# Starting the hybrid mixers from unnormed x, with fp32r forget gates: a six-layer transformer stack on one core

## The reference, cut to what matters

```python
x = x + hybrid_mixer(rms_norm_2(x, mix_norm[l]), w_in[l], lb_all[l], hgrn_out_norm[l], fox_f_bias[l], w_out[l])

z = h @ w_in                       # 1024 x 3592, h = x * rsqrt(mean(x*x) + eps) * mix_norm
hq, hf, hi, hg, fq, fk, fv, ff = split(z)          # 4 x 512, 3 x 512, 8
logf_h = logaddexp(log(lb), log1p(-lb) + log_sigmoid(hf))
k_h = (1 - lb) * sigmoid(-hf)
o_h = hgrn2_chunk_scan(silu(hq), k_h, hi, logf_h)  # 4 heads, gated linear attention
o_h = rms_norm_2(o_h, out_norm_w) * silu(hg)
logf_f = log_sigmoid(ff + fox_bf)
o_f = forgetting_attention(fq, fk, fv, logf_f)     # 8 heads, causal softmax with decay
return concat(o_h, o_f) @ w_out
```

## Time and profile before

| | |
|---|---|
| median of 3 runs | 2643.28 us (2640.35 to 2643.76) |
| profiled execution | 2639.53 us, its span 2637.8 us |
| mean granted TensorE clock | 0.997 of 2.4 GHz |
| TensorE busy | 2578.1 us, 98% of the span |
| VectorE, ScalarE, GpSimd busy | 63%, 51%, 6% |
| hybrid 0 / hybrid 1 begin | at about 1601 / 2183 us of the span |

### The profile page before, as it was taken

One profiled execution on the slowest core, in us unless ns is written; L12 is line 12 of the kernel. 1 busy time (PEld: TensorE's weight loads), 2 busy tenths in 40 slices (PEclk: granted clock), 3 DMA queues, 4 the chain that ended last, 5 costly groups with the idle time before them and its releaser, 6 DMA issues.

```text
span 2637.8 us, 48807 instructions
## 1 busy us (share of the span) xinstructions
PE 2578.1 (98%) x21538; PEld 2516.6 (95%) x21538; DVE 1668.8 (63%) x1988; ACT 1357.2 (51%) x1687; POOL 163.0 (6%) x259
## 2 busy tenths in 40 slices
PE   8999999999999999999999999999999999999998
PEld 8989999899998999999999999999999999999998
DVE  5667556575586655676646656756656657764764
ACT  5745445554456544665535445555445436544543
POOL 4400000000020000420000000000000000000000
PEclk9999999999999999999999999999999999999999
DMA  7515565456554664533666765444766755344763
GB/s 215 170 33 160 193 239 164 144 180 224 181 168 148 193 240 148 155 122 118 206 240 171 195 225 169 135 154 136 198 195 185 196 194 161 113 136 138 195 196 128
DMA packets 430995, 452.43 MB, mean 172 GB/s; under 512 B 14114, under 2 KB 395792, under 8 KB 428608
## 3 DMA queue, kind: packets, MB, share of 16 engines
q1 hardware_dynamic: 417952, 416.05, 50.6%
q0 software_dynamic: 8336, 32.87, 3.6%
q10 hardware_dynamic: 4496, 0.39, 0.1%
HBM read 441.15 MB, written 7.60 MB: 170 GB/s over the span
## 4 chain that ended last, share of the span: by engine, by line
PE 85%; DVE 6%; ACT 6%; DMA 1%; issue 1%; POOL 1%; ACTq 0%; SPq 0%; DVEq 0%
PE ps L621 84%; ACT wH L1517 2%; DVE wL L2167 2%; ACT hidden_parts L1577 1%; DMA ring<-in_gdn_w_in 0%; DVE arena L2742 0%; ACT L1544 0%; POOL arena L508 0%; PE ps L1052 0%; DVE hT L2423 0%; POOL arena L510 0%; PE ps L1270 0%; DVE sq L2250 0%; DVE arena L2431 0%; DMA arena<-leaf_out 0%
## 5 line engine op out<-in xcount | busy, mean ns | idle before, releaser
L2167 DVE TENSOR_TENSOR wL<-ring,wH 128x2048 fp32r<-128x2048 f32 x392 | 898.6, 2293 | 744.6 <-ACT wH L1517 744.2
L1517 ACT ACTIVATE wH<-ring 128x2048 fp32r<-128x2048 f32 x392 | 753.6, 1922 | 988.8 <-PE ps L621 986.6
L621 PE MATMUL ps<-hidden_parts,wH 128*128 128x256 f32 x6656 | 989.5, 277 | 3.8 <-ACT hidden_parts L1577 2.8
L621 PEld LDWEIGHTS ps<-hidden_parts,wH 128*128 128x128 f32 x6656 | 899.6, 188 | 5.9 <-issue 3.6
L621 PE MATMUL ps<-hidden_parts,wL 128*128 128x256 f32 x3328 | 693.2, 276 | 1.5 <-DVE wL L2167 1.5
L621 PEld LDWEIGHTS ps<-hidden_parts,wL 128*128 128x128 f32 x3328 | 521.9, 188 | 1.8 <-DVE wL L2167 1.8
L621 PE MATMUL ps<-hH,wH 128*128 128x256 f32 x2624 | 366.1, 281 | 6.4 <-DVE hH L2184 3.1
L621 PE MATMUL ps<-hH,wL 128*128 128x256 f32 x2624 | 358.9, 278 | 3.5 <-DVE wL L2167 3.5
L621 PE MATMUL ps<-hL,wH 128*128 128x256 f32 x2624 | 347.7, 279 | 0.0
L621 PEld LDWEIGHTS ps<-hH,wH 128*128 128x128 f32 x2624 | 329.1, 189 | 12.6 <-issue 10.5
L621 PEld LDWEIGHTS ps<-hH,wL 128*128 128x128 f32 x2624 | 326.9, 188 | 4.3 <-DVE wL L2167 4.3
(11 more groups left out here) (324 smaller groups left out, 1971.7 us busy)
## 6 DMA issues: line engine op xcount, KB each, us to landing
ring<-in_mlp_w SPq DMA_DIRECT2D x128, 1024.0 KB, 5.4
ring<-in_ffn_w_gate SPq DMA_DIRECT2D x88, 512.0 KB, 4.0
ring<-in_ffn_w_up SPq DMA_DIRECT2D x88, 512.0 KB, 5.3
ring<-in_ffn_w_down SPq DMA_DIRECT2D x44, 1024.0 KB, 5.0
ring<-in_gdn_w_in SPq DMA_DIRECT2D x32, 1024.0 KB, 5.9
ring<-in_w_in SPq DMA_DIRECT2D x28, 1024.0 KB, 5.4
hidden_parts<-mem_parts POOLq DMA_DIRECT2D x14, 1024.0 KB, 6.9
ring<-in_mlstm_w_in SPq DMA_DIRECT2D x12, 1024.0 KB, 5.3
```

What stands on the lines that cost most here:

```text
L621: return pe.matmul(o, l, r, start=start, stop=stop, **k)
L1517: f(wH[:, n % PARTS, :], ring[:, n % RING, :], ACT.Copy).then_inc(sem("high_split"), 1)
L2167: tt(wL[:, n % PARTS, :], ring[:, n % RING, :], wH[:, n % PARTS, :].bitcast(F32), ALU.subtract)\
```

## The change

Both hybrid parts begin as cross does. `late_start` (ScalarE) copies x times the norm weights to fp32r and `late_low` (VectorE) makes its low part, in `start_x`, two stretches of the arena that later hold `gate` and `v_tok`. The first four slabs and the forget gates are made from start_x; the sum of squares is finished between the products of the second slab (`behind_high`). Products of the four slabs are multiplied by rs as VectorE takes them out of their banks (`scaled_out`, instead of ScalarE's copies; Silu is then done in place). The normed h, high and low, is made later (`normed`, `normed_high`, `normed_low`), for the fifth slab on. The forget gates become an fp32r product of three parts with the gate columns split (`fox_w`), multiplied by rs before the bias. The fifth slab's low half stands ahead of the forget gate's chain in VectorE's order, no longer behind the rows. In hybrid 0 all 48 filler matmuls go before the first product. POOL clears the upper part of `gate` only when the fourth slab is done.

```diff
         floorH, floorL = hH[:, 0, :], hL[:, 0, :]
+        start_x = (hidH[:, 24:32, :], hidH[:, 16:24, :])
+        fox_w = [flat_parts[:, at:at + DC * 8].rearrange("p (c n) -> p c n", c=DC) for at in (15424, 15488)]
         x_rows = v_tok
...
...
                     W.chain(pool.memset(qk[64:128, 12:16, :], 0.0))
+                    pool.wait_ge(sem("products_done"), group("w_in_2", i, HYBRID_ORDER[3]))
                     W.chain(pool.memset(gate[0:64, 4:8, :], 0.0))
...
...
-            def first_products(name, layer, js, c, at, src=(hH, hL), together=True):
+            def first_products(name, layer, js, c, at, src=(hH, hL), together=True, behind_high=None):
...
...
                     both_halves(1, high_w[1], xL, k)
+                if behind_high:
+                    behind_high()
                 pe.wait_ge(sem("low_split"), n[1] + 1)
...
...
             def hybrid(l):
-                norm_sum(behind=6, filler=filled_before[("hybrid", l)], at=(0, 0, 0, 0, 10))
-                first_products("w_in_2", l, HYBRID_ORDER[0:2], DC, columns)
+                fill(filled_before[("hybrid", l)], 0, 2 * MEM_PIECES)
+                first_products("w_in_2", l, HYBRID_ORDER[0:2], DC, columns, src=start_x,
+                               together=False, behind_high=summed_norm)
                 filler_out(filled_before[("hybrid", l)])
...
-                        pe.wait_ge(sem("gates_in"), GATE_LOADS)
-                        for k in range(DC):
-                            last = mm(ps[0:8, 0, 0:T], gw[:, 3 + l, k, 0:8], hT[:, k, :], k == 0, k == DC - 1)
+                        pe.wait_ge(sem("gate_split"), W.next("gate_split"))
+                        last = three(ps[0:8, 0, 0:T], [lambda k: fox_w[0][:, k, :], lambda k: fox_w[1][:, k, :]],
+                                     [lambda k: start_x[0][:, k, :], lambda k: start_x[1][:, k, :]], DC)
                         last.then_inc(sem("gates_done"), 1)
                     if n >= 4:
-                        pe.wait_ge(sem("evac"), W.next("evac"))
-                    (to_tokens if s in (4, 5) else to_channels)("w_in_2", l, s, bank_of(n))
+                        pe.wait_ge(sem("scaled_out"), W.next("scaled_out"))
+                    if n == 4:
+                        pe.wait_ge(sem("normH_ready"), W.next("normH_ready", 4))
+                        pe.wait_ge(sem("normL_ready"), W.next("normL_ready", 4))
+                    (to_tokens if s in (4, 5) else to_channels)("w_in_2", l, s, bank_of(n),
+                                                                src=start_x if n < 4 else (hH, hL))
                 to_channels("w_in_2", l, 8, 1)
...
...
                 empty_filler(filler)
+
+            def late_start(name, layer, j, gain, k0, filler):
+                for c in range(4):
+                    act.wait_ge(sem("x_ready"), W.next("x_ready"))
+                    for k in (2 * c, 2 * c + 1):
+                        ins = f(start_x[0][:, k, :], xT[:, k, :], ACT.Copy, scale=column(gain, k0 + k))
+                    ins.then_inc(sem("hH_ready"), 1)
+                empty_filler(filler)
+                split(slab_no[(name, layer, j)] + PARTS)
+                for c in range(4):
+                    f(sq[:, 2 * c:2 * c + 2, :], xT[:, 2 * c:2 * c + 2, :], ACT.Square).then_inc(sem("xsq_ready"), 1)
+                ln_exp()
+                act.wait_ge(sem("ss_ready"), W.next("ss_ready"))
+                rsqrt(ps[:, 2, 0:T], rs[:, :], D, "rs_ready")
+
+            def normed_high():
+                for c in range(4):
+                    act.wait_ge(sem("h_ready"), W.next("h_ready", 2))
+                    f(hH[:, 2 * c:2 * c + 2, :], hT[:, 2 * c:2 * c + 2, :], ACT.Copy).then_inc(sem("normH_ready"), 1)
...
...
             def hybrid(l):
-                x_norm("w_in_2", l, HYBRID_ORDER[0], filler=filled_before[("hybrid", l)])
-                channels("w_in_2", l, 1, 4, chunks(qk, 4))
-                act.wait_ge(sem("evac"), W.next("evac", 2))
+                late_start("w_in_2", l, HYBRID_ORDER[0], "mix_norm_2", l * DC, filled_before[("hybrid", l)])
+                for n in range(2):
+                    ready("w_in_2", l, HYBRID_ORDER[n])
+                act.wait_ge(sem("scaled_out"), W.next("scaled_out", 2))
                 W.chain(f(glog, qk[:, 4:8, :], ACT.Abs))
...
                 f(glog, glog, ACT.Ln, bias=1.0).then_inc(sem("glog_ready"), 1)
+                normed_high()
                 act.wait_ge(sem("fz_ready"), W.next("fz_ready"))
...
...
                 f(qk[:, 4:8, :], qk[:, 4:8, :], ACT.Sigmoid, scale=-1.0).then_inc(sem("hk_ready"), 1)
-                channels("w_in_2", l, 0, 6, chunks(qk, 0), func=ACT.Silu)
+                for s in range(2):
+                    ready("w_in_2", l, s)
+                    act.wait_ge(sem("scaled_out"), W.next("scaled_out"))
+                    v = qk[:, 2 * s:2 * s + 2, :]
+                    f(v, v, ACT.Silu)
                 channels("w_in_2", l, 3, 4, chunks(gate, 0), func=ACT.Silu)
...
...
                         attention_slab(SLAB_ENDS[n - 1])
-                W.next("evac", 12)
                 square_pair(0, two(ps[:, 0, :]), "o_ready")
...
...
-            def late_low(gain, k0, x_parts, name, layer):
+            def late_low(gain, k0, x_parts, name, layer, j=0):
                 for c in range(4):
...
                     ins.then_inc(sem("hL_ready"), 1)
-                split(slab_no[(name, layer, 0)] + PARTS)
+                split(slab_no[(name, layer, j)] + PARTS)
                 sum_squares("xsq_ready", "xsq_summed")
+
+            def normed(gain, k0):
+                for c in range(DC):
+                    stt(hT[:, c, :], xT[:, c, :], column(gain, k0 + c), rs[:, :], ALU.mult, ALU.mult)\
+                        .then_inc(sem("h_ready"), 1)
+
+            def normed_low():
+                dve.wait_ge(sem("h_ready"), W.next("h_ready", DC))
+                for c in range(4):
+                    dve.wait_ge(sem("normH_ready"), W.next("normH_ready"))
+                    v = slice(2 * c, 2 * c + 2)
+                    tt(hL[:, v, :], hT[:, v, :], hH[:, v, :].bitcast(F32), ALU.subtract)\
+                        .then_inc(sem("normL_ready"), 1)
...
...
             def hybrid(l):
-                x_norm("mix_norm_2", l * DC, "w_in_2", l, HYBRID_ORDER[0])
+                late_low("mix_norm_2", l * DC, start_x, "w_in_2", l, HYBRID_ORDER[0])
+                dve.wait_ge(sem("gates_in"), GATE_LOADS)
+                W.chain(dve.tensor_copy(fox_w[0], gw[:, 3 + l, :, 0:8]))
+                tt(fox_w[1], gw[:, 3 + l, :, 0:8], fox_w[0].bitcast(F32), ALU.subtract).then_inc(sem("gate_split"), 1)
                 if l == 0:
...
                 r = lambda k: rows[0:8, k, :]
+
+                def scaled_out(n):
+                    s = HYBRID_ORDER[n]
+                    dve.wait_ge(sem("products_done"), group("w_in_2", l, s))
+                    c = 2 * s if s < 2 else 4 + 2 * (s - 2)
+                    tt(qk[:, c:c + 2, :], two(ps[:, 4 + n, :]), rs_twice(), ALU.mult).then_inc(sem("scaled_out"), 1)
+
+                refill("w_in_2", l, HYBRID_ORDER[0])
+                dve.wait_ge(sem("rs_ready"), W.next("rs_ready"))
+                scaled_out(0)
+                scaled_out(1)
+                normed("mix_norm_2", l * DC)
                 refill("w_in_2", l, 3)
                 dve.wait_ge(sem("gates_done"), W.next("gates_done"))
-                ts(r(1), ps[0:8, 0, 0:T], gbias[:, 2 + l:3 + l], None, ALU.add).then_inc(sem("fz_ready"), 1)
+                W.chain(tt(r(1), ps[0:8, 0, 0:T], rs[0:8, :], ALU.mult))
+                ts(r(1), r(1), gbias[:, 2 + l:3 + l], None, ALU.add).then_inc(sem("fz_ready"), 1)
+                normed_low()
+                refill("w_in_2", l, 0)
                 dve.wait_ge(sem("glog_ready"), W.next("glog_ready"))
...
...
                 negative_cum(r(5)).then_inc(sem("rows_ready"), 1)
-                refill("w_in_2", l, 0)
+                scaled_out(2)
+                scaled_out(3)
                 if l:
```

## The result

| | before | after |
|---|---|---|
| median of 8 runs each, us | 2644.47 (2640.35 to 2648.22) | 2651.58 (2648.12 to 2652.96) |
| profiled execution, us (span) | 2639.53 (2637.8) | 2648.12 (2646.4) |
| mean granted clock | 0.997 | 0.993 |

The changed kernel is slower: ratio 1.0027, 95% interval 1.0017 to 1.0037, or 7.1 us between the medians. The forecast was +8.2 us (2651.5). The interval goes from 4.5 to 9.8 us, so the times alone don't tell the forecast from its rival without a fall of the clock (+4.8); the traces and experiment 2 have to. That 2651.5 lies within 0.1 of the median is partly luck: the change was 1.1 smaller than forecast, and eight runs put the kernel before 1.2 higher than the three that the forecast started from.

A forecast was written before the change was run, and what follows sets the result against it. The prediction took VectorE's queue up to the sixth slab's low half to set the pace: 3.5 in hybrid 1, 1.3 in hybrid 0 and 3.4 for the clock make +8.2 on 2643.3, 2651.5 us; range 2645 to 2656.

The forecast's parts named there:

- rival without a fall of the clock: Both hybrids: the low clock falls into the pauses or not at all; +4.8 us, 2648.1; chance 0.26.
- The start: Start of each hybrid: first product 1.77 us behind the residual, as in cross; worth 5.6 and about 3.6 of TensorE's time.
- The gates: Forget gates: 24 fp32r matmuls take 2.7 us, ceiling 5.4; neither end matters to the sum if VectorE sets the pace.
- VectorE's queue, hybrid 1: Walk of VectorE's instructions from rs to the sixth slab's low half, ending at 2227.3 against 2223.77.
- The term +3.5: Hybrid 1: the sixth slab's low half ends 3.5 us later than before.
- Hybrid 0: Sixth low half ends at 1645.9, where TensorE started on it at 1644.6 before: 1.3 us later.
- The waits: TensorE at the sixth slab: stands 4.7 us in hybrid 0; some 5 in hybrid 1, then again after 16 matmuls.
- The clock: Behind each hybrid's pause the granted clock falls to 1.2 GHz: 2 x 1.7 = 3.4 us, bounds 0 and 5.
- The sum: Whole kernel: +4.8 us from the later sixth low halves plus 3.4 for the clock, +8.2, 2651.5 us.
- moved fifth low half: VectorE's queue, hybrid 1: 2.2 us behind a wait of 0.9; the stretch after the first forget instruction loses those 2.2.
- moved clears: POOL's clearing waits for the fourth slab; used only by the attention, nothing sooner queued behind it, so no cost.

The follow-up runs named there:

- experiment 2: Changed kernel with matmuls of ones, whose result nothing uses, filling TensorE's pauses ahead of the sixth slab and its low half; 2646.52 us, ratio 1.0015 to the kernel before.
- experiment 5: Kernel before with the changed forget gates alone, keeping its normed start and its lists; 2639.03 us, ratio 0.9988 to the kernel before.
- experiment 7: Changed kernel with the forget gates' matmuls done twice and GpSimd's clears waiting for two more slabs' products; 2646.49 us, ratio 1.0020 to the kernel before.
- experiment 1: Changed kernel with the 24 forget-gate matmuls done twice in each hybrid part; 2655.87 us, ratio 1.0039 to the kernel before.
- experiment 9: Changed kernel with the fifth low half back behind the rows and GpSimd's clears behind two more slabs' products; 2643.74 us, ratio 1.0003 to the kernel before.
- two variants: Changed kernel with the gates' matmuls done twice (ratio 1.0039), and changed kernel with the fifth low half back behind the rows (ratio 1.0026).
- experiment 8: Kernel before with the changed forget gates, old normed start, and slab halves put in order of need; 2643.01 us, ratio 1.0004 to the kernel before.
- experiment 4: Changed kernel with slab halves made in the order TensorE needs them on ScalarE and VectorE; 2635.50 us, ratio 0.9969 to the kernel before.
- experiments 5 to 8: Old start with new gates (0.9988); changed kernel with fifth low half back (1.0026); gates twice, clears later (1.0020); old start, halves in order (1.0004).

## Why the prediction was right, point by point

- **The start.** Forecast +1.77 behind the residual, by cross; measured +1.77. rs forecast at +12.8 and +17.7, measured +12.8 and +17.6 (1616.44 - 1598.88).
- **The gates.** Forecast 2.7, measured 2.94, in the changed kernel and in experiment 5. From the first gate matmul to the next product it is 2.77 and 2.78: width 8 streams at the slabs' rate, and the 2.94 counts the end of the last one. As the forecast said, neither end matters once VectorE sets the pace (experiment 7, and experiment 1 in part 0).
- **VectorE's queue, hybrid 1.** The third high half at +14.7 forecast, +14.6 measured (2198.49); the wait for the fifth 0.9 forecast, 0.78 measured; the fifth low half done at +29.8 and +29.7; the sixth at +44.6 and +44.1. The term +3.5 measured 3.0. Of the 0.5, 0.35 lie in the stretch from the fifth low half on, which the walk had too long.
- **Hybrid 0.** The low half was to be 1.3 later than TensorE came for it before; it is 0.9 later (44.76 against 43.90).
- **The waits.** Forecast 4.7 in part 0, and some 5 and a second one in part 1; measured 4.34, then 4.73 and 2.06. TensorE's arrival at the sixth slab in part 1 was +33.7 and +33.7.
- **The clock.** Forecast 1.7 in each part, from the earlier trace rows. Measured 7.9 - 3.0 - 0.9 = 4.0 in both parts together (2.2 in part 0, 1.8 in part 1), against 3.4, and experiment 2 gave back 3.5 when the pauses were filled. The trace agrees with the rule of the Trainium skill (TensorE: Matmul & The Clock Gate, "The HAM clock gate") that stood beside that estimate: idle, then 1.2 GHz (0.50 from 2222), then released (1.00 from 2232).
- **The sum.** 3.5 + 1.3 + 3.4 = 8.2 forecast, 3.0 + 0.9 + 4.0 = 7.9 at the seventh slabs, 7.1 between the medians. The queue's terms were 0.9 too large, the clock's 0.6 too small; that they nearly cancel is luck, the mechanism of each is not.
- **What it did not say.** Two things that the forecast summed over. It priced the moved fifth low half as one item in a list; it is 5.7 of the 7.9 us (experiment 9), as long as the sixth slab's halves stay where they were. And it took the moved clears as free, since nothing is queued behind them. That held only by luck of 0.15 us: they ended at 2214.55 and the steps that they can hold began at 2214.70. In two variants, which shift one against the other, they cost 1.7 and 2.1 us.

**Where the start's gain went.** It wasn't undone by contention or given back later. Both kernels meet at the same instruction of VectorE, and 5.6 us less of TensorE in front of it only lengthened TensorE's wait. With the halves in order of need part of the gain is there: against the old start with the same gates (experiment 5) the seventh slab comes 2.8 and 4.7 us earlier and the tree 2.8 in both parts, 5.6 us in all and 5.0 by the ratios, of the 9.5 by which the first products come earlier (5.6 in part 1, and 3.9 in part 0: +6.8 in place of +10.7). The new start needs that order, and the old one does not profit from it (experiment 8). What is left to have: in part 1 of experiment 4 the seventh slab is 5.5 us earlier than before and the tree only 3.3 (58.1 against 61.4). Waits of 0.76 and 0.68 lie in between, and the starts of the groups of eight show what they cost with the slower matmuls just behind them: 1.83, 1.02, 1.78 and 1.05 from one to the next (2230.09 to 2235.77) where 0.91 is usual, 2.1 of the 2.2. No kernel tried to have those waits back.

## What to carry to other kernels

Before making the busiest engine's way to a meeting point shorter, walk the other engines' queues to that same point; if one of them arrives last after the edit, the edit buys a pause, and the pause may cost a spell at half clock on top. Order the pieces that another engine waits for by when it will need them after the edit: here the order was worth 15 us, and the shorter start 5 us with that order and less than nothing without it. An instruction that waits in the middle of an in-order queue charges its wait to all that stand behind it, so a half that is moved forward must have its input by then.

## What the runs showed of the hardware that was not expected

- GpSimd's clears of 0.95 to 0.98 us hold VectorE's tensor-scalar instructions from SBUF to SBUF: 0.35 us each alone, up to 1.12 under a clear, four of them 2.79 and 3.24 instead of 1.14. The longest is about one clear plus a little. Not every instruction of VectorE is held: in the changed kernel the low half at 2211.24 and the step at 2213.45 lie over the same clears and take their usual 2.29 and 1.22. The Trainium skill (SBUF — State Buffer, "Who interferes with whom") has a rule for this: such an instruction of VectorE can, under conditions on its operands, take a pair of ports that GpSimd shares, whoever begins first keeps it for the whole instruction, and the other stands. The times agree with it. That the clears hold the steps is shown by moving them (experiments 7 and 9); the ports themselves no run shows.
- The clock's falls are not fixed to the program. The same pauses in code that both kernels share had a fall in one execution (740 to 750 before, 2410 to 2420 after) and none in the other. At 1.7 us each, a handful of them moves one execution by 5 us, as much as the effect studied. The profiled execution of experiment 2 took 2653.53 with full clock in both hybrids, 7 us over its own median. The Trainium skill (TensorE: Matmul & The Clock Gate, "What's actually happening") says that the number of slow matmuls at a kernel's start differs from run to run of the same kernel; here the mean granted clock of one kernel differs between its runs too (0.993 to 0.997 in the 35 runs of the kernel before beside experiments 5 to 8).
- fp32r matmuls with 8 columns of weights take as long as ones with the full 128: 24 of them 2.77 to 2.78 us from the first to the next product (experiment 5: 2202.05 to 2204.82), 0.116 each, against 0.115.
